# Softmax with the keys on the partitions: the turning of the probabilities is taken out of an attention stage

## The reference, cut to what matters

```python
def mla_attend(qn, qr, kn, kr, v):
    s = jnp.einsum('bqhd,bkhd->bhqk', qn, kn) + jnp.einsum('bqhr,bkr->bhqk', qr, kr)
    p = jax.nn.softmax(s.astype(jnp.float32) * MLA_SCALE, axis=-1).astype(v.dtype)
    return jnp.einsum('bhqk,bkhd->bqhd', p, v)

# in token_mixer: queries of x see all 768 keys, queries of the context see the 256 of the context
    o_x = mla_blockwise(qn_x, qr_x, jnp.concatenate([kn_c, kn_x], 1), jnp.concatenate([kr_cc, kr_x], 1),
                        jnp.concatenate([vv_c, vv_x], 1))
    ...
    o_c = mla_attend(qn_c, qr_c, kn_c, kr_cc, vv_c).reshape(bsz, uc.shape[1], MLA_HEADS * V_HEAD)
```

## Time and profile before

| what | us |
|---|---|
| median of 3 runs | 3390.55 |
| lowest and highest of them | 3390.54, 3394.94 |
| the profiled execution's own time | 3387.16 |
| its span on the core | 3385.4 |
| TensorE busy | 3254.8 |
| VectorE busy | 1832.8 |
| ScalarE busy | 1193.2 |
| GpSimd busy | 1088.5 |

### The profile page before, as it was taken

How to read it: one execution, slowest core, us unless ns; L and a number is a source line. 1 busy time by engine, 2 the same in 40 slices (tenths; PEclk the granted TensorE clock), 3 DMA queues, 4 the chain that set the end, 5 groups by cost and what they waited for, 6 DMA issues and landing times. The chain is left out here.

```text
span 3385.4 us, 50809 instructions
## 1 busy us (share of the span) xinstructions
PE 3254.8 (96%) x19092; PEld 2659.0 (79%) x19092; DVE 1832.8 (54%) x2865; ACT 1193.2 (35%) x1793; POOL 1088.5 (32%) x542
## 2 busy tenths in 40 slices
PE   5999999999999999999999999999999979999998
PEld 4888667788888888888776677778888857788886
DVE  2869444613268242245997454138333576777634
ACT  2233244631244232233542446234322364323223
POOL 2433100432232322322441004443444424344442
PEclk8999999999999999999999999999999989999999
DMA  6222245022221222222322332332333221233332
GB/s 186 63 61 55 48 139 168 13 63 56 62 69 57 63 63 63 63 63 59 91 75 47 113 113 54 90 93 75 94 94 94 87 68 57 81 93 93 95 98 75
DMA packets 549141, 270.30 MB, mean 80 GB/s; under 512 B 55922, under 2 KB 547146, under 8 KB 548827
## 3 DMA queue, kind: packets, MB, share of 16 engines
q1 hardware_dynamic: 547330, 267.20, 27.8%
q10 hardware_dynamic: 889, 0.30, 0.0%
q0 software_dynamic: 736, 0.17, 0.0%
HBM read 265.50 MB, written 2.10 MB: 79 GB/s over the span
## 5 line engine op out<-in xcount | busy, mean ns | idle before, releaser
L374 POOL TENSOR_TENSOR weights_low<-weight_ring,weights_high 128x1024 fp32r<-128x1024 f32 (+1 forms) x407 | 972.9, 2392 | 1754.9 <-ACT weights_high L365 1754.3
L365 ACT ACTIVATE weights_high<-weight_ring 128x1024 fp32r<-128x1024 f32 (+1 forms) x408 | 410.1, 1005 | 1126.1 <-PE ps L475 1044.0
L470 PE MATMUL ps<-features_high,weights_high 128*128 128x512 f32 (+1 forms) x1888 | 640.2, 354 | 4.7 <-DVE features_low L2276 4.6
L471 PE MATMUL ps<-features_low,weights_high 128*128 128x512 f32 (+1 forms) x1888 | 636.7, 353 | 0.0
L470 PEld LDWEIGHTS ps<-features_high,weights_high 128*128 128x128 f32 x1888 | 356.2, 189 | 64.3 <-DVE features_low L2276 6.0
L471 PEld LDWEIGHTS ps<-features_low,weights_high 128*128 128x128 f32 x1888 | 355.8, 188 | 55.2 <-issue 0.2
L475 PE MATMUL ps<-features_high,weights_low 128*128 128x512 f32 (+1 forms) x1888 | 384.9, 351 | 0.0
L470 PE MATMUL ps<-u_high,weights_high 128*128 128x512 f32 (+2 forms) x944 | 367.6, 393 | 12.5 <-ACT weights_high L365 5.5
L471 PE MATMUL ps<-u_low,weights_high 128*128 128x512 f32 (+2 forms) x944 | 361.1, 387 | 0.0
L475 PEld LDWEIGHTS ps<-features_high,weights_low 128*128 128x128 f32 x1888 | 305.5, 188 | 47.3
L1249 DVE SCALAR_TENSOR_TENSOR conv<-conv,vectors 128x512 f32<-128x512 f32 (+1 forms) x480 | 305.9, 707 | 1.2 <-DVE conv L1157 0.9
(11 more groups left out here) (585 smaller groups left out, 4953.7 us busy)
## 6 DMA issues: line engine op xcount, KB each, us to landing
weight_ring<-in_w_in SPq DMA_DIRECT2D x262, 256.0 KB, 3.2
weight_ring<-in_w SPq DMA_DIRECT2D x256, 256.0 KB, 3.0
weight_ring<-in_w_mod SPq DMA_DIRECT2D x192, 256.0 KB, 3.8
weight_ring<-in_w_up SPq DMA_DIRECT2D x88, 256.0 KB, 3.1
weight_ring<-in_w_out SPq DMA_DIRECT2D x48, 256.0 KB, 3.1
weight_ring<-in_w_down SPq DMA_DIRECT2D x32, 256.0 KB, 3.1
weight_ring<-in_w_mla_out SPq DMA_DIRECT2D x32, 128.0 KB, 2.3
weight_ring<-in_w_conv_out SPq DMA_DIRECT2D x32, 128.0 KB, 2.2
```

What stands on the lines that cost most here:

```text
L365: act.activation(core.ring_high[:, split_slot(run, q), 0:n], core.ring[:, slot, 0:n], ACT.Copy).then_inc(core.high_ready.sem, 1)
L374: pool.tensor_tensor(core.ring_low[:, split_slot(run, q), 0:n], core.ring[:, (run.first + q) % SLOTS, 0:n], high.bitcast(F32), ALU.subtrac ...
L470: pe.matmul(to, w_high[:, k, 0:m], high(k, a, b), start=(first and k == ks[0]), stop=False, skip_group_check=True)
L471: pe.matmul(to, w_high[:, k, 0:m], low(k, a, b), start=False, stop=False, skip_group_check=True)
```

## The change

Scores are made with the keys on the partitions: 128 keys by 512 queries of one head, in six steps for each head pair (`i` from 0 to 5). In the first layer a seventh step holds the context's queries. The exponentials then already stand as the product with the values wants them, and nothing is turned.

The maxima must be known beforehand. They come from rough scores, with queries and keys rounded to `fp32r` and the queries on the partitions (`unit`). ScalarE makes the rounded copies. VectorE takes the maxima. TensorE turns them into rows of 512 (`turn_rows`). ScalarE copies a row under the queries, as their row 96, and the keys have a row of ones there, which GpSimd writes along with the rotated part. The product of scores thus has 97 rows and comes out with the maximum taken off.

VectorE adds the tiles of exponentials up (`add`). TensorE sums the added tile over the partitions with a product with ones (`total`). VectorE takes the reciprocal of 128 x 512 numbers and multiplies the attended values with it (`divided`). The units of a head pair run within the steps of the pair before, those of the first pair in the head part. Rows of each head pair are turned in the last step of the pair before. The modulation groups hang on the steps (`mod_steps`).

The diff, cut to its core. Lines that it takes out stand in the kernel before and are not repeated:

```diff
+    probs = [core.ranks[:, at + n * TX:at + (n + 1) * TX] for n in range(4)]
+    sums = [core.ranks[:, at + (4 + j) * TX:at + (5 + j) * TX] for j in range(2)]
+    ctx_sums = [core.rope[:, j * TC:(j + 1) * TC] for j in range(2)]
+    round_keys, round_queries = ([tile[:, j, 0:T] for j in range(2)] for tile in (core.ring_high, core.ring_low))
...
+    steps_of = [(p, i) for p in range(PAIRS) for i in range(items)]
+    units = [(j, r) for j in range(2) for r in range(NTX)] + ([(j, NTX) for j in range(2)] if both else [])
+    n_rows = 4 if both else 2
+    adds_of_pair = 2 * (items - 1)
+    def unit_at(p, i, j):
+        u = 2 * (i - 1) + j
+        return u if p + 1 < PAIRS and 0 <= u < len(units) else None
+    def adds_until(p, i, j):
+        return p * adds_of_pair + 2 * (max(i, 1) - 1) + j + 1
+    mod_steps = [g for g, (p, i) in enumerate(steps_of) if i < NT and (both or i % 3 != 2)]
     assert 2 * len(mod_steps) == n_mods
...
+        def unit(p, u):
+            j, r = units[u]
+            n = p * len(units) + u
+            if r in (0, NTX):
+                pe.wait_ge(s["rounded"].sem, s["rounded"].at(4 * p + (2 * j + 2 if p else j + 3)))
+            if n:
+                pe.wait_ge(s["max_ready"].sem, s["max_ready"].at(n))
+            if both and p >= 2 and u == 0:
+                pe.wait_ge(s["attended_copied"].sem, s["attended_copied"].at(2 * (p - 1)))
+            if r < NTX:
+                for a, b in parts(T):
+                    mm = pe.matmul(rough[:, a:b], round_queries[j][0:QH, r * P:(r + 1) * P], round_keys[j][0:QH, a:b],
...
+        def turn_rows(p, ctx):
+            pe.wait_ge(s["max_ready"].sem, s["max_ready"].at((p + 1) * len(units) if ctx else p * len(units) + 2 * NTX))
+            for x in range(2 * ctx, 2 * ctx + 2):
+                j, lo = x % 2, x // 2 * NTX
+                for r in range(lo, NT if lo else NTX):
+                    mm = pe.matmul(rows[x * 32:(x + 1) * 32, (r - lo) * P:(r - lo + 1) * P],
+                                   small_max[:, j, r:r + 1].to_broadcast([P, 32]), core.ident, start=True, stop=True,
+                                   skip_group_check=True)
+                mm.then_inc(s["rows_turned"].sem, 1)
...
+        project_keys(0, None)
+        project_keys(1, None)
+        pe.wait_ge(s["kr_copied"].sem, s["kr_copied"].at(2))
+        unit(0, 0)
+        project_keys(2, 1)
+        unit(0, 2)
+        project_keys(3, 3)
+        unit(0, 4)
         for t in range(NT):
             if t == 0:
...
+        def score(g, j):
+            p, i = steps_of[g]
+            if g:
+                pe.wait_ge(s["exp_ready"].sem, s["exp_ready"].at(2 * g - 1 + j))
+            elif j == 0:
+                pe.wait_ge(s["v_copied"].sem, s["v_copied"].at(1))
+                pe.wait_ge(s["v_copied_by_act"].sem, s["v_copied_by_act"].at(1))
+            if i == 0:
+                pe.wait_ge(s["rows_copied"].sem, s["rows_copied"].at(n_rows * p + j + 1))
+                if j == 0:
+                    pe.wait_ge(s["kr_copied"].sem, s["kr_copied"].at(2 * p + 2))
+            if i < NT:
+                mm = pe.matmul(scores[j], keys_of[2 * p + j][0:QH + 1, i * P:(i + 1) * P], queries[j][0:QH + 1, p, 0:TX],
+                               start=True, stop=True)
+            else:
...
+        def total(p, ctx):
+            n = p * (2 if both else 1) + ctx
+            pe.wait_ge(s["added"].sem, s["added"].at(adds_until(p, NT if ctx else NT - 1, 1)))
             if n:
...
+        def attend(g):
+            p, i = steps_of[g]
+            n = p * (2 if both else 1)
+            pe.wait_ge(s["exp_ready"].sem, s["exp_ready"].at(2 * g + 2))
+            if g == 0:
                 pe.wait_ge(s["v_copied"].sem, s["v_copied"].at(3))
                 pe.wait_ge(s["v_copied_by_act"].sem, s["v_copied_by_act"].at(3))
...
+            if i < NT:
+                if i == 0 and p:
...
+        for g, (p, i) in enumerate(steps_of):
+            for j in range(2):
+                score(g, j)
+                u = unit_at(p, i, j)
+                if u is not None:
+                    if g == 1 and j == 0:
+                        pe.wait_ge(s["v_copied_by_act"].sem, s["v_copied_by_act"].at(3))
+                    unit(p + 1, u)
+                if i == items - 1 and p + 1 < PAIRS and (j == 0 or both):
+                    turn_rows(p + 1, j)
+            if g:
+                attend(g - 1)
+            if g in mod_steps:
+                b = mod_steps.index(g)
                 if b:
                     turn_mods(b - 1)
+                else:
+                    pe.wait_ge(s["v_copied"].sem, s["v_copied"].at(3))
                 mod_rows_pair(core, pe, run, *at_group("mod", 2 * b), mod_in)
...
+        def exponent(g, j):
+            p, i = steps_of[g]
+            act.wait_ge(s["scored"].sem, s["scored"].at(2 * g + j + 1))
+            if g >= 2:
+                act.wait_ge(s["attended"].sem, s["attended"].at(g - 1))
+                before, at = steps_of[g - 2]
+                act.wait_ge(s["added"].sem, s["added"].at(adds_until(before, at, j)))
+            act.activation(probs[(2 * g + j) % 4], scores[j], ACT.Exp).then_inc(s["exp_ready"].sem, 1)
...
+        def rounded(p, j):
+            act.wait_ge(s["rough_scored"].sem, s["rough_scored"].at(p * len(units)))
+            rounded_queries(p, j)
+            rounded_keys(p, j)
+        def row_copy(p, x):
+            j, ctx = x % 2, x // 2
+            act.wait_ge(s["rows_turned"].sem, s["rows_turned"].at(n_rows * p + x + 1))
+            n, lo = (TC, TX) if ctx else (TX, 0)
+            act.activation(queries[j][QH:QH + 1, p, lo:lo + n], rows[x * 32:x * 32 + 1, 0:n], ACT.Copy).then_inc(s["rows_copied"].sem, 1)
...
+        for g, (p, i) in enumerate(steps_of):
+            for j in range(2):
+                exponent(g, j)
+                if i < 2 and j == 1 and p + 1 < PAIRS:
+                    rounded(p + 1, i)
+                if g == 0 and j == 1 and both:
+                    row_copy(0, 2)
+                    row_copy(0, 3)
+                if i == items - 1 and p + 1 < PAIRS:
+                    if j == 0:
+                        row_copy(p + 1, 0)
+                        row_copy(p + 1, 1)
...
+        def maximum(p, u):
+            j, r = units[u]
+            dve.wait_ge(s["rough_scored"].sem, s["rough_scored"].at(p * len(units) + u + 1))
+            if r < NTX:
+                to, source = small_max[:, j, r:r + 1], rough
+            else:
+                to, source = small_max[:, j, NTX:NT], rough[:, 0:2 * TC].rearrange("p (n t) -> p n t", t=TC)
+            nc.vector.tensor_reduce(to, source, AX.X, ALU.max, negate=True).then_inc(s["max_ready"].sem, 1)
...
+            p, i = steps_of[g]
+            here = probs[(2 * g + j) % 4]
+            dve.wait_ge(s["exp_ready"].sem, s["exp_ready"].at(2 * g + j + 1))
+            if i == NT:
+                ins = nc.vector.tensor_tensor(ctx_sums[j], here[:, 0:TC], here[:, TC:2 * TC], ALU.add)
+            elif i == 1:
+                ins = nc.vector.tensor_tensor(sums[j], probs[(2 * g - 2 + j) % 4], here, ALU.add)
+            else:
+                dve.wait_ge(s["added"].sem, s["added"].at(adds_until(p, i - 1, j)))
+                ins = nc.vector.tensor_tensor(sums[j], sums[j], here, ALU.add)
+            ins.then_inc(s["added"].sem, 1)
+        def divided(p, ctx):
+            n = p * (2 if both else 1) + ctx
+            dve.wait_ge(s["totaled"].sem, s["totaled"].at(n + 1))
+            width, lo, source = (TC, TX, ctx_result) if ctx else (TX, 0, result)
+            if n:
+                dve.wait_ge(s["attended_copied"].sem, s["attended_copied"].at(n))
+            nc.vector.reciprocal(recip[:, 0:width], totals[:, 0:width]).then_inc(s["recip_ready"].sem, 1)
+            dve.wait_ge(s["recip_ready"].sem, s["recip_ready"].at(n + 1))
+            nc.vector.tensor_tensor(out[:, p, lo:lo + width], source, recip[:, 0:width], ALU.mult).then_inc(s["attended_copied"].sem, 1)
...
+        for g, (p, i) in enumerate(steps_of):
+            for j in range(2):
+                u = unit_at(p, i, j)
+                if u is not None:
+                    maximum(p + 1, u)
+                if i:
+                    add(g, j)
+            if g in mod_steps:
+                b = mod_steps.index(g)
                 dve.wait_ge(core.weights_used.sem, group_done(core, run, *at_group("mod", 2 * b + 1)))
                 nc.vector.tensor_copy(mod_rows, mod_in).then_inc(mod_copied.sem, 1)
+            if g and steps_of[g - 1][1] >= NT - 1:
+                divided(steps_of[g - 1][0], steps_of[g - 1][1] == NT)
+        divided(PAIRS - 1, both)
```

More of the change, by code:

```diff
@@ L1396, in attention_stage @@
     spot = lambda name: gemm(core, place[name])
-    v_bank = lambda t: bank(core, 4 + (t + 2) % 4, 512)
+    v_bank = lambda t: bank(core, (2, 3, 4, 5, 7, 1)[t], 512)
     def at_group(kind, n):
@@ L1409, in projected @@
```

(26 more changed lines are left out.)

153 lines of the change are left out of this document (73 added, 80 removed).

## The result

The changed kernel takes 3431.11 us, the median of 4 runs (3429.14 to 3435.74), beside 3392.6 for the kernel before, measured with it. The ratio is 1.0121, with a 95% interval of 1.0109 to 1.0133. It is slower, as forecast, but by 38.5 us where 25 were expected, and the time lies above the range, whose upper end was 3425.

The account below looks back on a forecast made before the run. The prediction took TensorE's own order of work to bound the kernel. It added 7.5 (first layer), 14.5 (second layer) and 3.4 us (clock), 25.4 in all, to 3387.2 and gave 3413, range 3390 to 3425.

Parts of the forecast that it names:

- the division: VectorE's reciprocals were to take 3.35 us for 512 numbers and 1.75 for 256, and make TensorE wait.
- rival 1: The reciprocal of 512 runs at a copy's pace, 0.69 us, leaving +3.1 us: 3390; chance 0.13.
- the sum at full clock: The two attention stretches summed without clock loss: 182.7 us in the first layer, 155.5 in the second.
- head parts: Key and value projections with the first pair's units and rows: 27.9 us in the first layer, 27.2 in the second.
- The waits of the changed kernel in the second layer: TensorE was to stand 3.5 us ahead of the second unit in pairs 1 and 2, 2.7 before the last pair's attending.
- The rows for x: Turning the maxima into rows on TensorE, eight products per head pair: 2.0 us with gaps; the context's four: 1.16.
- step 6 of the first layer: The step with scores, both row turnings, attending and the context's total: 6.9 us.
- step 1 of pairs 1 and 2: In the first layer, 6.6 us, with the second rough unit waiting 1.25 more than the usual 0.4.
- the clock: Five TensorE pauses of 2.7 us or more were to lower its clock, costing 3.4 us, between nothing and 8.
- the 3.4: The clock term's size in us, added to the growth of the two stretches.
- the 25.4: The whole predicted growth in us: 7.5 first layer, 14.5 second, 3.4 clock, added to the profiled execution's 3387.2.
- The rest of the kernel: Everything outside the two attention stretches was not to move.

Follow-up runs that it names:

- e1: The changed kernel with the reciprocals of 512 and 256 columns replaced by copies, the division left out: 3395.75 us, ratio 1.0013.
- e2: The changed kernel with throwaway products of 512 columns put on TensorE where it waits for the division: 3412.59 us, ratio 1.0059.
- e9: The changed kernel with one throwaway product before the first rough unit of step 1, in pairs 1 and 2 of the first layer only: 3427.74 us.
- e8: The kernel before with two throwaway reciprocals of 256 columns ahead of the first maximum in pairs 1 to 3, both layers: 3413.02 us, ratio 1.0055.
- e10: The kernel before with two throwaway reciprocals of 218 columns ahead of the first maximum in pairs 1 to 3, both layers: 3406.29 us, ratio 1.0050.
- e5: The changed kernel with the loops of `turn_rows` exchanged, so that the two heads' column groups take turns: 3424.12 us, ratio 1.0091.
- e3: The changed kernel with each step's second rough unit moved behind the attending and its maximum behind the additions: 3414.19 us, ratio 1.0065.

## Why the prediction was right in direction and wrong in size

**Right: what bounds, and the division.** TensorE sets the time, and VectorE's reciprocals are its delay: 3358 and 1750 ns as estimated. e1 shows that rival 1 named the deciding term: with a short instruction in the division's place the median is 3395.75, where the rival had 3390.

**Right: the sum at full clock.** e2 gives both stretches without a lowered clock, 182.6 and 155.0, for 182.7 and 155.5. Its parts fit too: head parts 27.8 and 27.3 (27.9 and 27.2 predicted); the first layer's pair 0 36.7 (36.7) and its pairs 1 and 2 40.0 each (40.0); the second layer's pair 0 28.7 (28.4) and its pairs 1 and 2 32.8 each (33.1). The waits of the changed kernel in the second layer are 3.03 and 3.02 (3.5) and 2.60 (2.7).

**Two terms in it were off and cancelled, which was luck.** The rows for x took 1.46 us and the context's 0.57, for 2.0 and 1.16: I had taken the upper bound of the streams and added gaps. The step that holds both, step 6 of the first layer, took 6.0 us for 6.9. The other term is step 1 of pairs 1 and 2, which took 7.2 us in e2 for 6.6. The wait there came one unit earlier: in the first layer `unit` waits for `attended_copied` at the first unit of the pairs from 2 on (`p >= 2 and u == 0`), since the rough bank is the bank of the context's result. That line stands in the diff, and I read past it. The pause is nearly as long as the one that I had in front of the second unit (1.60 for 1.65), but the second unit then waits for its maximum as in every other step.

**The step that failed: the clock.** "The change makes five pauses of 2.7 us or more" and "I count 3.4 us in all, between nothing and 8". In the two stretches it is 13.9 us (changed kernel less e2): pairs 1 and 2 of the first layer took 42.7 and 43.1 for the 40.0 of the sum and of e2, so 2.7 and 3.1 more with 6.8 us at half clock in each. Three things were wrong in the term. First, pauses under 2.7 can count too: 1.60 us, with 0.62 a little ahead of it, was followed by 6.8 us at half clock, twice. e9 took both away by filling 1.0 us of each. Second, what follows a pause was read from 2.5 us after one pause. The next 2.5 us of that trace have a clock of 0.68:

```profile
2067.00:2069.50 2.50, 2.50 (x9) 1.93 (x9) 2.46 (x6) 1.78 (x3) 0.00 (x0) 0.68 0.00 0
```

So the half clock behind that pause cost 0.9 and 0.8 us, 1.7 together. Third, the 3.4 has no working: five times the 0.9 of the earlier trace rows is 4.5, and five times 1.7 is 8.5. The stretches at half clock that followed here are 3.4 to 10.2 us long. Half of each is lost if TensorE has work: half of 33.9 is 17.0, more than the 13.9. That the difference lies in VectorE's waits, which shrink while TensorE is slower, is my reading and isn't shown.

**The base of the forecast was low too.** I added the 25.4 to the profiled execution, 3387.2, which lay under every timed run of its kernel beside it, and called the 3.4 to the median within what runs differ by. The median beside the change is 3392.6, so 5.4 of the 18.1 between 3413 and 3431.11 were the base.

**The rest of the kernel did move.** I wrote that it would not. The time from the first stage to the second, before and after:

```profile
589.50:1871.50 1282.00, 1259.21 (x6980) 1064.01 (x6981) 680.39 (x1086) 442.47 (x654) 394.95 (x191) 1.00 0.22 61
```

```profile
603.43:1891.57 1288.14, 1265.20 (x6980) 1069.62 (x6981) 680.22 (x1086) 443.53 (x654) 394.92 (x193) 0.99 0.22 60
```

TensorE has the same 6980 instructions and is busy for 6.0 us longer, with 24.1 us at half clock where there were 10.2. Of these 13.9 more, 3.6 are the rest of the half-clock stretch that began in the pauses at the stage's end, and e2, which filled them, has none there. The others stand some 70, 471 and 1209 us behind the stage, in code that the change doesn't touch. Half clock stands at 70 and 1209 (within 5 us) in the kernel before too, in other lengths, and at 471 in every run here but that of the kernel before. e8 and e10 have 23.9 us in this time and 1286, though their program is the old one and their stage ends like that of the kernel before; e2 has 13.7 and 1282.7. So most of it doesn't stand at the stage's end, and what sets the lengths stays open. Behind the second layer 6.9 us more have 65.5 us at half clock for 53.8; half of that difference is 5.9, and 1.0 stays open.

In the profiled executions the 48.6 us are thus 35.2 in the stretches, 6.1 between them, 6.9 behind and 0.3 ahead. In the medians, 38.5, I can't divide them, since each kernel has one profile.

**What stays open.** What decides whether half clock follows a pause, and for how long. The same pauses of 0.62 and 1.60 us were followed by 6.8 us each in the changed kernel, by 3.4 each in e5 and by none in e3. Those of 1.79 us were followed by half clock in the first layer of e10 and not in the second. And the same second layer had 17.1 us in the changed kernel and 23.9 in e9. So e1 and e2 show what the pauses and the half clock cost as a whole, but what a single pause will cost can't be told beforehand from these runs.

## What to carry to other kernels

A pause on TensorE costs its length and, behind it, up to half of the time that the clock stays down: price both, take the second from several pauses of the same kernel as a range with zero in it, and don't set a least length by one row. Put the sum on the median, not on the profiled execution. A row or tile of numbers to be divided is the expensive shape for a reciprocal: divide what is short (2 to 24 numbers per partition took 0.15 to 0.30 us, 512 took 3.36) and spread it by a product, or cut the division up so that what TensorE waits for can go between. When a wait of a new function stands in the diff, follow it to the bank that it guards, in each layer.

## What the runs showed of the hardware

- The reciprocal on VectorE takes 6.56 ns a number per partition (3358 ns for 512), where the maximum of 768 takes 1.25 (957 ns): 5.3 times as long. The Trainium skill, "VectorE: DVE Perf Modes", First, the fixed hardware budget, gives it a repeat count of 8. No row shows the repeats themselves; the time for each number is 5.3 times that of the maximum and not 8.
- Throwaway work on TensorE in its pauses made a kernel faster, by 18.5 us in e2.
- A pause of 1.60 us was followed by 6.8 us at 1.2 GHz twice (changed kernel), by 3.4 twice (e5) and by none twice (e3); one of 0.60 by none (e9, e2).
- Pauses made in the kernel before, without the change, were followed by half clock too: three of three in the first layer (e8 and e10), one of three (e8, 2.26 us) and none of three (e10, 1.79 us) in the second.
- Float32 products of 128 columns for two heads in different column groups: 91 ns a record in a row, 63 in turn.
